# Bias rows of a sliding-window attention: one eight-row product stored 128 times, in place of eight broadcast products

## The reference, cut to what matters

```
def sliding_window_attention(q, k, v, attn_sinks, rel_bias):
    ...
    s = jnp.einsum("bnqhgd,bnkhd->bnhgqk", qb, kb).astype(jnp.float32) * scale
    qi = jnp.arange(BLOCK)[:, None]
    kj = jnp.arange(2 * BLOCK)[None, :]
    dist = qi + BLOCK - kj
    in_band = (dist >= 0) & (dist < WINDOW)
    bucket = t5_causal_bucket(jnp.maximum(dist, 0))
    bias = rel_bias.astype(jnp.float32)[bucket]
    ...
    s = jnp.where(valid[None, :, None, None], s + bias, -jnp.inf)
```

## Time and profile before

| | |
|---|---|
| median of 3 runs | 2169.43 us |
| lowest and highest of the 3 | 2164.5 and 2172.26 us |
| span of the profiled execution, first to last instruction | 2161.6 us |
| PE busy | 2121.7 us, 98% of the span |
| DVE busy | 1442.4 us, 67% |
| ACT busy | 858.3 us, 40% |
| mean granted PE clock | 0.996 |

### The profile page before, as it was taken

How to read it: one execution, slowest core, us unless ns; L and a number is a source line. 1 busy time by engine, 2 the same in 40 slices (tenths; PEclk the granted TensorE clock), 3 DMA queues, 4 the chain that set the end, 5 groups by cost and what they waited for, 6 DMA issues and landing times.

```text
span 2161.6 us, 29125 instructions
## 1 busy us (share of the span) xinstructions
PE 2121.7 (98%) x10648; PEld 1837.8 (85%) x10648; DVE 1442.4 (67%) x2713; ACT 858.3 (40%) x1306; POOL 1038.6 (48%) x573
## 2 busy tenths in 40 slices
PE   8989999999999999999999999999999999999999
PEld 7857888888877877899999999999998888888887
DVE  5973411110054995369998777787867999999987
ACT  4354522232264454253334444444433333333332
POOL 1203244443423333435566888888863444444342
PEclk9999999999999999999999999999999999999999
DMA  4202344444442222334347899998899999999996
GB/s 177 82 27 62 104 117 127 117 119 115 117 118 74 86 71 77 117 106 121 112 147 207 242 267 321 284 315 249 261 309 318 388 388 371 373 375 377 369 359 251
DMA packets 240489, 444.14 MB, mean 205 GB/s; under 512 B 102459, under 2 KB 152028, under 8 KB 240220
## 3 DMA queue, kind: packets, MB, share of 16 engines
q1 hardware_dynamic: 152060, 299.07, 41.8%
q0 software_dynamic: 55488, 134.83, 19.3%
q10 hardware_dynamic: 32800, 8.39, 1.8%
HBM read 397.71 MB, written 44.50 MB: 205 GB/s over the span
## 4 chain that ended last, share of the span: by engine, by line
PE 69%; POOL 13%; DVE 8%; issue 4%; DMA 3%; ACT 2%; SPq 0%; DVEq 0%; ACTq 0%; POOLq 0%
PE bank L469 22%; PE bank L473 22%; PE bank L472 22%; POOL gate_matrices L1151 9%; POOL y L1160 4%; DMA y<-in_peer_u_rows,gidx 3%; DVE m L1979 1%; PE bank L923 1%; DVE xn L1980 1%; DVE WL L2297 1%; PE bank L645 1%; DMA wraw<-in_peer_u 1%; ACT sc L1302 1%; DVE y L2308 0%; DVE hots L2329 0%
## 5 line engine op out<-in xcount | busy, mean ns | idle before, releaser
L1140 POOL TENSOR_TENSOR WL<-wraw,WH 128x1024 fp32r<-128x1024 f32 x171 | 435.9, 2552 | 723.5 <-ACT WH L1191 723.5
L1191 ACT ACTIVATE WH<-wraw 128x1024 fp32r<-128x1024 f32 x411 | 435.0, 1060 | 627.4 <-PE bank L469 393.6
L469 PE MATMUL bank<-XH,WH 128*128 128x384 f32 (+2 forms) x1864 | 668.8, 359 | 12.6 <-DVE WL L2297 7.8
L473 PE MATMUL bank<-XH,WL 128*128 128x384 f32 (+2 forms) x1864 | 657.8, 353 | 0.0
L472 PE MATMUL bank<-XL,WH 128*128 128x384 f32 (+2 forms) x1864 | 657.6, 353 | 0.0
L469 PEld LDWEIGHTS bank<-XH,WH 128*128 128x128 f32 x1864 | 351.4, 189 | 46.3 <-issue 12.9
L472 PEld LDWEIGHTS bank<-XL,WH 128*128 128x128 f32 x1864 | 351.6, 189 | 29.0 <-issue 0.7
L473 PEld LDWEIGHTS bank<-XH,WL 128*128 128x128 f32 x1864 | 351.1, 188 | 28.7
L2297 DVE TENSOR_TENSOR WL<-wraw,WH 128x1024 fp32r<-128x1024 f32 x240 | 293.0, 1222 | 57.6 <-ACT WH L1191 51.8
L469 PE MATMUL bank<-WH,GH 128*128 128x512 f32 x768 | 298.9, 389 | 1.6 <-issue 1.6
L473 PE MATMUL bank<-WH,GL 128*128 128x512 f32 x768 | 298.8, 389 | 0.0
(11 more groups left out here) (313 smaller groups left out, 2561.8 us busy)
## 6 DMA issues: line engine op xcount, KB each, us to landing
wraw<-in_peer_u SPq DMA_DIRECT2D x128, 512.0 KB
wraw<-in_peer_v SPq DMA_DIRECT2D x128, 512.0 KB
activations<-ac SPq DMA_DIRECT2D x122, 192.0 KB
ar<-activations SPq DMA_DIRECT2D x122, 192.0 KB
gr<-gate_matrices SPq DMA_DIRECT2D x124, 128.0 KB
wraw<-in_w_gate SPq DMA_DIRECT2D x22, 512.0 KB
wraw<-in_w_up SPq DMA_DIRECT2D x22, 512.0 KB
wraw<-in_w_down SPq DMA_DIRECT2D x22, 512.0 KB
```

The costliest lines, as they stand in the source:

```text
L469: mm = pe.matmul(out, wh, xh, start=first, stop=False)
L473: return pe.matmul(out, wl, xh, start=False, stop=last)
L1140: pool.tensor_tensor(WL[:, u % NW, 0:m], wraw[:, u % NR, 0:m], WH[:, u % NW, 0:m].bitcast(F32), ALU.subtract).then_inc(s("w_lo"), 1)
L1191: act.activation(WH[:, u % NW, 0:k * n], wraw[:, u % NR, 0:k * n], ACT.Copy).then_inc(s("w_hi"), 1)
```

## The change: what it does

The table `relb` is used as the weights directly, so one product gives eight rows (8 partitions x 384), one per head, instead of eight products with 128 equal rows each. `relbB` and DVE's copy into it go. ACT makes one copy of 8 x 384 instead of eight of 128 x 384. The store still writes all of `skew_rows` (128 x 8 x 384, 1.57 MB), but reads it from eight partitions: for each head the same 384 numbers are read 128 times (a step of zero), and the head is the outermost dimension on both sides. The read back is the same. PE waits for the table's two semaphores itself, and the wait of DVE's first reciprocal on the fill of row 33 goes.

```diff
-            relbB = sb("relbB", [BUCKETS + 1, NH, P], F32, sc)
...
-        brow = sc1[:, :, :, :].rearrange("p a h n -> p (a h n)")[:, 0:NH * SKEW].rearrange("p (h n) -> p h n", h=NH)
+        brow = sc1[:, :, :, :].rearrange("p a h n -> p (a h n)")[0:NH, 0:SKEW]
...
             def bias_rows():
-                pe.wait_ge(s("relb_spread"), 1)
-                for h in range(NH):
-                    out = take("brow", h)
-                    full(pe.matmul(out[:, 0:SKEW], relbB[:, h, :], oneh[:, :], start=True, stop=True), "brow", h)
+                pe.wait_ge(s("relb_padded"), 1)
+                pe.wait_ge(s("relb_landed"), 32)
+                out = take("brow", 0)
+                full(pe.matmul(out[0:NH, 0:SKEW], relb[:, :], oneh[:, :], start=True, stop=True), "brow", 0)
...
-            for h in range(NH):
-                wait_read(sp, ("brow", h))
-            sp.dma_start(skew_dram, brow[:, :, :]).then_inc(s("skew_out"), 16)
+            wait_read(sp, ("brow", 0))
+            sp.dma_start(skew_dram.rearrange("p h m -> h p m"), brow.unsqueeze(1).to_broadcast([NH, P, SKEW])).then_inc(
+                s("skew_out"), 16)
             sp.wait_ge(s("skew_out"), 16)
             back = bass.AP(skew_dram.tensor, P - 1, [[NH * SKEW - 1, P], [SKEW, NH], [1, 2 * P]])
             sp.dma_start(biasT[:, :, :], back).then_inc(s("bias_landed"), 16)
...
             def bias_rows():
-                for h in range(NH):
-                    src = wait_full(act, ("brow", h))
-                    act.activation(brow[:, h, :], src[:, 0:SKEW], ACT.Copy).then_inc(frees(("brow", h)), 1)
+                src = wait_full(act, ("brow", 0))
+                act.activation(brow, src[0:NH, 0:SKEW], ACT.Copy).then_inc(frees(("brow", 0)), 1)
...
-                dve.memset(relb[BUCKETS:BUCKETS + 1, :], NEG).then_inc(s("dve_link"), 1)
-                links[0] += 1
-                dve.wait_ge(s("dve_link"), links[0])
+                dve.memset(relb[BUCKETS:BUCKETS + 1, :], NEG).then_inc(s("relb_padded"), 1)
...
-                dve.wait_ge(s("relb_landed"), 32)
-                dve.tensor_copy(relbB[:, :, :], relb[:, :].unsqueeze(2).to_broadcast([BUCKETS + 1, NH, P])).then_inc(
-                    s("relb_spread"), 1)
```

## The result

The changed kernel takes 2194.6 us (median of 4 runs, 2190.16 to 2198.07), the kernel before 2167.18 us (4 runs, 2164.5 to 2172.26): 1.0121 times as long, with an interval of 1.0096 to 1.0146, 27.4 us. The profiled execution took 2192.96 us, its span is 2191.2 us, 29.6 us longer than that of before.

A forecast was written before the change was run, and what follows sets the result against it. PE, busy 98%, and DVE, nearly as late, were taken to bound the start, with the store on unit 6's path. Attention at 92.15 + 31.4, 18.1 us later, gave 2179.7, plus 7.8 for the runs' median 2187.5 us; range 2164 to 2197.

The forecast's parts named there:

- (a): Bias products at the start: seven products and copies go, PE gains some 9.8 us, unit 5 ends at 49.2.
- (b): Store of the bias rows: issued at 33.9 instead of 40.6, after ACT's one copy.
- (c): The store's own time: 31.4 us instead of 5.1, eight neighbouring partitions sharing two ways out; chance 0.62 for 26 to 36.
- X: The store's time from issue to landing: 5.1 us before the change, 31.4 predicted.
- a choice between 5.1 and 61.4: Bounds for the store's time: only engines limit it (5.1 us), or eight partitions share one way out (61.4 us).
- The rival of eight engines: Store limited by eight transfer engines, not partitions: store time 8.9 us, attention 4.3 us earlier, 2165.1 us; chance 0.12.
- (d): Path behind the store: unit 6's remainder 8.2 us after landing, then DVE's 50.05 us to the attention.
- the same run of 50.05 us: DVE from unit 6's remainder to the attention: works without a wait, as long as before the change.
- the turning point: The store time that decides whether the change gains or loses: predicted at 13.2 us.
- (e): PE idle from 49.2 for 25 us, maybe restarting at half clock; costs at most 0.1 us, hidden behind DVE's taps.
- The sum: Attention begins at 123.5 against 105.4, 18.1 us later; profiled execution 2179.7 us, runs' median 2187.5 us.
- the range: Final time for 8 in 10: 2164 to 2197 us; for the likeliest case alone, 2178 to 2196.

The follow-up runs named there:

- both placings: Changed kernel with the eight rows on every second partition (2178.64 us) or every fourth (2172.7 us), one run each.
- with POOL held: Changed kernel with POOL's remainder of unit 14 held until DVE's second chunk of taps is done; 2202.69 us.
- with 12 KB rows: Kernel before, its store reading the 12 KB rows from partitions 0 to 7 alone, 16 times each; 2202.01 us.
- with the later read back: Changed kernel with SP's wait for the store and the read back moved behind unit 11's load; 1.0071 times the time of before.
- the last kernel: Changed kernel with rows on every fourth partition and the read back moved behind unit 11's load; median 2164.95 us, 0.9973 of before.

## Why the prediction was right, and which term was mis-sized

**(a) The products that go.** Right. One product of two passes takes 0.75 us at 32.38, the clock stays at its upper level over 32.4 to 49.3, and PE is through with unit 5 at 49.7 (49.2 predicted).

**(b) The store's start.** 33.66 us, 33.9 predicted.

**(c) X.** Right, 32.75 us for 31.4, and by the mechanism that was chosen: two fours of partitions at 25 GB/s each. The trace of before could not show it, because there all fours and all engines worked at once; the placing of the rows in two, four and eight fours does. By the rows alone the two was a choice between 5.1 and 61.4 that came true, not a reading. The table of the Trainium skill ("SBUF — State Buffer", section "Door 1: The DMA port swizzle") that spoke against the change has four neighbours behind one port and 27.6 GB/s for it. The runs agree with the grouping, and their 24 to 25 GB/s per four lie about a tenth below its rate.

The rival of eight engines fell as the cause of X: the outermost dimension was 8 in the change and in both placings, and X was 32.75, 18.07 and 10.09. The store does seem to run on eight engines, by its eight small packets (16 before) and by the halves of the loads that passed it; but out of two and four fours these wait for the partitions. At every fourth partition the store runs at 200 GB/s, 25 for each four and as much for each of eight engines; there the two limits can't be told apart.

**(d) What waits for X.** Right up to unit 6: 42.1 + 32.75 = 74.85 by the prediction's line, 74.72 measured. The mis-sized term is "the same run of 50.05 us" behind it: it took 54.25 (74.72 to 128.97). The prediction took it from an execution in which POOL lost to DVE. The run is 50.04 and 49.97 us with every second partition and with POOL held, and 54.25 to 54.27 in the change, with every fourth partition, with 12 KB rows, with the later read back and in the last kernel. It has two lengths, and which one comes depends on whether POOL gets in between two taps. In the profiles POOL lost where it came within some 0.1 us of a tap's start and won where it came later into one; that is a pattern in the nine profiles with POOL free, not a rule that a run tested. It moves the turning point as well: with 54.25 us, X = 9.0 decides the sign, and the kernel with X = 10.09 begins its attention 0.25 us later than before.

The reason named for the wait was only half of it. The prediction spoke of the load's place behind the read back in SP's list; without that wait the load was still there only after 33.7 us, behind the store in its queue. For the sum this made no difference, for the cure it did.

**(e) PE.** Right. It stands idle from 49.66 for 26.43 us, comes back at a mean clock of 0.53 over 74.7 to 81.0, and DVE does not wait for its scores at 128.97.

**The sum.** 18.1 us at the attention were predicted, 23.6 came: 4.2 from the longer run, 1.35 from X, and the small terms. Behind the attention the two profiled executions differ by another 6.0 us (2062.2 for 2056.2), and the median lies 3.4 us over the span where the prediction added 7.8. So 5.5 and 6.0 more, less 4.4, make the 7.1 us between 2187.5 and 2194.6. The 4.4 hang on which execution was profiled and so, it seems, do most of the 6.0; that they go against each other is luck. For the 6.0 a reciprocal of DVE some 620 us behind the attention says so, here before and then in the changed kernel:

```profile
728.92 0.18 DVE L2013 RECIPROCAL st<-st 128x4 f32<-128x4 f32 x1
```

```profile
752.62 0.18 DVE L2006 RECIPROCAL st<-st 128x4 f32<-128x4 f32 x1
```

The changed kernel is 23.70 us late there, hardly more than the 23.59 at the attention; the other 5.9 come behind this mark, in work that the change leaves as it is. That stretch took 1432.7 us in the profile of before, 1435.3 to 1441.2 in eight others and 1448.0 with POOL held. The whole part behind the attention took 2056.2 to 2066.7 us in nine of the ten profiles and 2075.7 with POOL held, with PE's work in it nearly the same; the profile of before is at its short end. With POOL held the mark lies 627.7 us behind the attention instead of 623.5, so 4.2 of its 19.5 us over the profile of before come ahead of the mark. What sets the rest from one execution to the next stays open. The 23.6 us at the attention lie within the interval of the runs, 20.8 to 31.6 us.

In the range one step is a microsecond off (5 us around 2182 to 2192 are 2177 to 2197, not 2178 to 2196); nothing rests on it.

## What to carry to other kernels

A store that reads few neighbouring partitions many times is priced by the groups of four partitions it reads, not by its bytes alone: spread the rows so that each lies in its own four, which cost one copy of 0.16 us here and took X from 32.75 to 10.09 us. A slow transfer holds back the loads behind it in its queue, even if nothing waits for it, so count those loads before its own waiter, and see which of them can be issued ahead of it. A run of one engine's work that is copied from a profile is only as fixed as its neighbours: look in the same stretch for another engine that stretched its own operation to make it so.

## What the runs showed of the hardware

Eight rows in two, four and eight fours of partitions left at about 50, 97 and 200 GB/s, with packets of 1.5 KB, which took 213, 113 and 65 ns each; with 12 KB packets from two fours it was 49.

DVE's taps, with two inputs in on-chip memory, and POOL's remainder, which reads there too, shut each other out: one tap took 2.14 us longer while POOL worked for 2.61 us, or POOL took 11.54 us and the taps nothing more. The Trainium skill has this as an exclusive lock held for a whole instruction ("SBUF — State Buffer", section "SBUF: two separate sides"). The longer tap agrees with it; that a loser can wait through a dozen taps in a row is what the rows of before add.

A load whose issue began 0.35 us behind the store's in the same queue was there for ACT 33.7 us later: the issue took 8.96 us, and of the packets one half ran beside the store, the other behind it. With the store in another queue, a load issued behind it was there 17.9 us later, while the store still ran. The Trainium skill says that each transfer engine takes a queue's work in order and goes round between queues by packets ("DMA: Bandwidth & Descriptors", section "Queues, rings and completion order"); both runs agree.
